# Value pages issued from GpSimd's queue, and value products spread over half projection tiles

## The chip, the cores and the metric

One Trainium2 chip, one core of it. The metric is the time of one execution on the device, in microseconds (us); lower is better. Engines are named as in the profile: PE (TensorE), DVE (VectorE), ACT (ScalarE), POOL (GpSimd), SP (SyncE, which here only issues DMAs).

## What is computed

One inference step of a hybrid decoder layer: 1024 prompt tokens, and 8 sample rows of one token, each of which has 4096 past tokens in a paged cache (32 pages of 128 tokens). The part that the change touches is this, cut from the reference:

```python
z = rmsnorm(x) @ w_in                      # one combined projection, split into heads
# group A, prompt: causal differential attention, 8 heads
s1 = einsum('bqhd,bshd->bhqs', q1, k1) * scale; s2 = einsum(... q2, k2) * scale
out = einsum('bhqs,bshd->bqhd', softmax(s1) - lam * softmax(s2), v)
# group A, sample: the same over 32 gathered pages of cache_diff_k and cache_diff_v per row
# group B: an indexer (4 heads of 64) scores all tokens, top 256 are kept, attention over those
rel = relu(einsum('bqhd,bsd->bqhs', qi, ki)); score = einsum('bqhs,bqh->bqs', rel, wi)
_, idx = lax.top_k(score, 256)
```

After it come group B's attention, the output projection and the gates. Everything is float32.

## The kernel before

The program is a chain of stages with a barrier between them. The change lies in the second one, which takes from about 262 to 1909 us of the profile. It runs in nine **slots**, s = 0 to 8. Slot s projects head s of group A for the prompt (slot 8: group B's keys and values), and does three other things beside that projection: the prompt attention of head s-1, the score products of sample row s with its 32 key pages and its indexer keys, and the value products of sample row s-1 with its 32 value pages.

A slot is cut into eight **tiles** t = 0 to 7 of 128 prompt tokens. In tile t PE does `scores` (L1277) of the attention, then the projections of two blocks, each in two halves (`half`, L1244, eight k-steps, 16 matmul records), then `output` (L1297), with `probabilities` (L1288, transposes) and `values` (L1316, the products with one value page) between them. Where the value products stand is set by the table `VALUES`. Names used below for the places in a tile: **a** is behind the first half of the first block, **b** behind its second half, **c** behind the first half of the second block, **d** at the tile's end behind `output`. Before, a row of the table gives the products at b, at c and at d.

Value pages sit in a ring of three buffers (`ring_v`), key pages in a ring of four (`ring_k`). A value page v waits on `v_used[v % 3]`, which PE raises behind the products of page v-3. A key page p waits on `k_used[p % 4]`, which DVE raises behind the reduction of page p-4. SP issues both, in one program order: behind key page i+4 comes value page i+3, then the next pair, with the weights of the next slot and the stores between them. So when SP stands at a value page whose buffer PE still holds, the key pages behind it wait too.

On DVE, `page(s, p)` multiplies key page p with the query (L958; for 12 of 32 pages POOL does it, L794) and then reduces page p-1 (L962) and the index product of page p-1 (L965). How many pages a tile does is in `PAGES`: in slots 1 to 7 tiles 1 to 7 do 5, 5, 6, 4, 4, 5 and 3 pages. The first page of a tile stands between `maxima` (L1078, of the scores) and `combine` (L1087 to L1090, which needs the exponentials from ACT); the others behind `combine` and, in tiles 1 to 4, behind `update`, five short steps of a bisection for group B's threshold.

On POOL, product u of the indexer keys (L800) waits on `q_free[u % 2]`, which DVE raises behind the reduction of product u-2:

```python
if 16 * s + u // 2:
    pool.wait_ge(q_free[u % 2], 16 * s + u // 2)
pool.tensor_tensor(kprod[:, u % 2, :, :], kib[:, j % 2, :, :], ...).then_inc(q_rdy[u % 2], 1)
```

The bisection takes 31 rounds; a round is one `counts` on ACT (L858, six passes) and one `update` on DVE. `ROUNDS_IN` spreads them over the slots. After the last, DVE does `settle` and one `select` for each tile from 2 to 7. `turned` (L840) on ACT copies the transposed queries and keys of the next slot out of PSUM; the next slot's `scores` wait for it.

## Time and profile before

| | us |
|---|---|
| median of 3 runs | 3952.08 (3949.98 to 3962.9) |
| the profiled execution, its own time | 3954.57 |
| its span, first to last instruction | 3952.8 |
| slots 1 to 7 of the stage, 432.3 to 1736.5 | 1304.2 |
| slot 8, 1736.5 to 1898.1 | 161.6 |

The profiled execution stands 2.5 us above the median, within the spread of the runs. A timeline row gives the start, the length, the engine, the line, the output and inputs, the count, and in brackets how long the engine had been idle and what ended that. A row of windows gives the stretch, its length, the busy time of PE, PE's weight loads, DVE, ACT and POOL, each with its count of instructions, the granted TensorE clock as a share of full speed, the share of DMA time in use, and GB/s.

### The profile page before, as it was taken

The numbers are of one execution on the slowest core, as the hardware profiler recorded it, in microseconds if no ns is written. First come the engines' busy times: TensorE is split into PE (matmuls) and PEld (weight loads), VectorE is DVE, ScalarE is ACT, GpSimd is POOL, SyncE is SP. The second block draws the span as 40 slices with busy tenths as digits, with TensorE's granted clock in tenths as the row PEclk, the third lists the DMA queues.
The fourth block names the chain that finished last, engine by engine and source line by source line (L and its number), as shares of the span: only waits on it lengthen the run. The fifth ranks groups of instructions, "written<-read, shape, count | busy, mean of one in ns | idle before, by whom it ended". The sixth has DMA issues, their size and how long they took to land. (4 is left out here: it accounts for less than half of the span.)

```text
span 3952.8 us, 46957 instructions
## 1 busy us (share of the span) xinstructions
PE 3453.9 (87%) x16995; PEld 2339.6 (59%) x17025; DVE 1497.0 (38%) x2771; ACT 820.3 (21%) x1798; POOL 514.0 (13%) x480
## 2 busy tenths in 40 slices
PE   4969789898988888889358699999979999899999
PEld 3757567676766666667223677777744444444443
DVE  2028666666666676654555111111110002311111
ACT  4011424141423333221000122222220001110000
POOL 0004333333333232310000200000000000000000
PEclk9989899998999999999669699999989999999999
DMA  9864676666666766754100211111041101310110
GB/s 341 253 192 145 189 259 195 226 213 223 222 224 217 226 224 200 242 163 135 53 0 9 77 27 28 27 28 27 10 156 43 43 22 53 113 59 32 59 59 22
DMA packets 344067, 497.51 MB, mean 126 GB/s; under 512 B 58913, under 2 KB 244538, under 8 KB 342674
## 3 DMA queue, kind: packets, MB, share of 16 engines
q1 hardware_dynamic: 338384, 481.67, 38.3%
q10 hardware_dynamic: 3922, 8.65, 0.6%
q0 software_dynamic: 1536, 4.20, 0.4%
q8 instruction: 141, 2.31, 0.2%
q14 instruction: 84, 0.69, 0.1%
HBM read 466.55 MB, written 27.90 MB: 125 GB/s over the span
## 5 line engine op out<-in xcount | busy, mean ns | idle before, releaser
L1244 PE MATMUL Z<-W,hT 128*128 128x256 f32 x4608 | 1063.8, 389 | 37.7 <-ACT qk L829 24.1
L1244 PEld LDWEIGHTS Z<-W,hT 128*128 128x128 f32 x4608 | 887.7, 196 | 165.3 <-ACT qk L829 26.5
L2138 PE MATMUL S<-W,hT 128*128 128x512 f32 x1408 | 646.1, 597 | 8.1 <-DMA hT<-oT_d 8.1
L2138 PEld LDWEIGHTS S<-W,hT 128*128 128x128 f32 x1408 | 264.9, 191 | 356.0 <-issue 346.9
L800 POOL TENSOR_TENSOR kprod<-kib,qib 128x256 f32<-128x256 f32 x256 | 231.5, 908 | 696.8 <-DVE srel L965 554.2
L962 DVE TENSOR_REDUCE sc<-big 128x16 f32<-128x1024 f32 x256 | 309.7, 1210 | 0.5 <-DVE isc L999 0.3
L2138 PE MATMUL Z<-W,hT 128*128 128x512 f32 x640 | 303.6, 592 | 0.0
L794 POOL TENSOR_TENSOR big<-big,qb 128x1024 f32<-128x1024 f32 x96 | 231.9, 2416 | 274.6 <-DMA big<-in_cache_diff_k_dram 274.6
L1316 PE MATMUL DB<-big,ex 128*4 128x256 f32 (+1 forms) x2112 | 150.7, 397 | 109.1 <-DMA big<-in_cache_diff_v_dram 108.9
L958 DVE TENSOR_TENSOR big<-big,qb 128x1024 f32<-128x1024 f32 x160 | 197.6, 1235 | 126.4 <-DMA big<-in_cache_diff_k_dram 123.5
L2138 PEld LDWEIGHTS Z<-W,hT 128*128 128x128 f32 x640 | 121.5, 190 | 153.0 <-issue 152.6
L1799 PE MATMUL Z<-W,hT 128*128 128x256 f32 x896 | 209.9, 395 | 0.0
L1799 PE MATMUL DB<-W,hT 128*128 128x256 f32 x896 | 198.8, 380 | 0.0
L1799 PEld LDWEIGHTS Z<-W,hT 128*128 128x128 f32 x896 | 176.5, 200 | 25.3
L1799 PEld LDWEIGHTS DB<-W,hT 128*128 128x128 f32 x896 | 168.1, 190 | 21.7
L1078 DVE TENSOR_REDUCE small<-S 128x1 f32<-128x256 f32 (+7 forms) x128 | 90.9, 752 | 224.7 <-PE S L1280 224.7
L858 ACT ACTIVATE vg<-isc,small 128x384 bf16<-128x384 f32 (+1 forms) x186 | 163.9, 881 | 22.5 <-DVE small L1008 14.9
L1969 DVE SCALAR_TENSOR_TENSOR vg<-Z,small,vg 128x128 f32<-128x128 f32 x64 | 22.4, 351 | 359.2 <-PE Z L1851 359.0
L872 ACT ACTIVATE e<-S,small 128x256 f32<-128x256 f32 (+7 forms) x128 | 93.6, 736 | 277.0 <-issue 275.3
L1316 PEld LDWEIGHTS DB<-big,ex 128*4 128x4 f32 (+1 forms) x2112 | 40.1, 85 | 176.9 <-DMA big<-in_cache_diff_v_dram 132.7
L1277 PE MATMUL S<-qkT 64*128 64x128 f32 (+3 forms) x576 | 107.0, 508 | 25.6 <-ACT qkT L840 23.3
L1277 PEld LDWEIGHTS S<-qkT 64*128 64x128 f32 x576 | 61.6, 237 | 89.5 <-issue 83.3
(539 smaller groups left out, 3305.5 us busy)
## 6 DMA issues: line engine op xcount, KB each, us to landing
big<-in_cache_diff_k_dram SPq DMA_DIRECT2D x256, 512.0 KB, 5.5
big<-in_cache_diff_v_dram SPq DMA_DIRECT2D x256, 512.0 KB, 5.0
W<-in_w_in_dram SPq DMA_DIRECT2D x27, 2048.0 KB, 10.0
W<-in_w_in_dram SPq DMA_DIRECT2D x52, 1024.0 KB, 7.3
W<-in_w_ple_gate_dram SPq DMA_DIRECT2D x16, 1024.0 KB, 5.1
W<-in_w_out_dram SPq DMA_DIRECT2D x12, 1024.0 KB, 5.1
kib<-in_cache_idx_k_dram SPq DMA_DIRECT2D x256, 32.0 KB, 2.3
hT<-oT_d SPq DMA_DIRECT2D x3, 2048.0 KB, 21.5
```

Of the source, the lines that this page charges most:

```text
L794: pool.tensor_tensor(ring_k[u % 4], ring_k[u % 4], qb[:, :], ALU.mult).then_inc(k_mul[u % 4], 1)
L800: pool.tensor_tensor(kprod[:, u % 2, :, :], kib[:, j % 2, :, :], spread(qib[:, h, :], 1, 4), ALU.mult).then_inc(q_rdy[u % 2], 1)
L858: act.activation(junkb(s, r)[:, 0:w], score(t), ACT.Sign, scale=-1.0, bias=thrf[:, t:t + 1], accum_out=ssum[:, t:t + 1]).then_inc(a_cnt, 1)
L872: act.activation(e12[:, j, 0:n], S[j][:, 0:n], ACT.Exp, scale=SC_A, bias=nmx[:, t, j:j + 1], accum_out=rsum[:, t, j:j + 1]).then_inc(s_fre ...
L958: dve.tensor_tensor(ring_k[p % 4], ring_k[p % 4], qb[:, :], ALU.mult).then_inc(k_mul[p % 4], 1)
L962: dve.tensor_reduce(sc[:, u, :], ring_k[u % 4].rearrange("p (g d) -> p g d", d=64), AX.X, ALU.add).then_inc(k_used[u % 4], 1)
L1078: last = dve.tensor_reduce(mx[:, t, j:j + 1], S[j][:, 0:n], AX.X, ALU.max)
L1244: mm = pe.matmul(Z[b][:, 0:CW], hT[:, k, t * P:(t + 1) * P], W[:, w, k, :], start=(k == 0), stop=(k == KT - 1))
L1277: pe.matmul(S[j][:, lo:hi], qkT[64 * j:64 * j + 64, 0, t * P:n], qkT[64 * j:64 * j + 64, 1, lo:hi], start=True, stop=(hi < n))
L1316: mm = pe.matmul(DB[32 * g:32 * g + 4, 0:256], ex[0:r, v, 4 * g:4 * g + 4], ring_v[v % 3][0:r, 256 * g:256 * g + 256], start=(v == 0), sto ...
L1799: mm = pe.matmul(PB[t % 2][:, 0:CW], hT[:, k, t * P:(t + 1) * P], W[:, u, k, :], start=(k == 0), stop=(k == KT - 1))
L2138: mm = pe.matmul(b, hT[:, k, t * P:(t + 1) * P], Wr[:, k, :], start=(k == 0), stop=(k == KT - 1))
```

## The change

It has five parts. (1) `VALUES` now has four places for each tile, a to d: two value products in tile 1 and five (1, 1, 1, 2) in each of tiles 2 to 7; before they stood in groups of two to four. (2) All value pages are issued from POOL's queue. In slots 1 to 7 the first three of a row stand at the slot's start; a later page v is issued ahead of the first index product u for which a planned time of page v-3 (`value_done`) is under the planned time of product u (`key_done`) less 0.8 of a tile. In slot 8 they are issued as buffers come free. (3) SP keeps the key pages, the index pages, the weights and the stores; the weights of the next slot and the key store stand at planned times. (4) Slot 0 does no bisection round where it did two, slot 8 does three where it did one; `settle` moves from tile 1 to tile 3 and `select(t)` to two tiles later, the last three all in tile 7. (5) `turned(0)` stands ahead of ACT's last copy of slot 0, and the semaphore of the value stores is split.

```diff
-        VALUES = ((0, 0, 0), (0, 0, 4), (2, 0, 3), (2, 0, 3), (0, 2, 3), (0, 2, 3), (0, 2, 3), (0, 2, 1))
-        ROUNDS_IN = (2,) + (4,) * (HA - 1) + (1,)
+        VALUES = ((0, 0, 0, 0), (0, 0, 0, 2)) + ((1, 1, 1, 2),) * 6
+        key_done = lambda s: [t + (0.35 if n == 0 else 0.5 + 0.5 * n / PAGES[s][t]) for t in range(NT) for n in range(PAGES[s][t])]
+        value_done = [t + 0.25 * (q + 1) for t in range(NT) for q in range(4) for n in range(VALUES[t][q])]
+        def transfers(s):
+            keys = [(u, 0, p + 4) for p, u in enumerate(key_done(s)) if p + 4 < NPG] if s < HA else []
+            return sorted(keys)
+        ROUNDS_IN = (0,) + (4,) * (HA - 1) + (3,)
...
             def _(sp):
...
-                    if s:
-                        for v in range(3):
-                            value_page(s - 1, v)
                     weights(s, 1)
...
-                    for i in range(NPG):
-                        if s < HA:
-                            if i % 4 == 0 and i + 4 < NPG:
-                                index_pages(s, i // 4 + 1)
-                            if i + 4 < NPG:
-                                key_page(s, i + 4)
-                        if s and i + 3 <= NPG:
-                            value_page(s - 1, i + 3)
-                        if i == 18 and s + 1 < SLOTS:
-                            weights(s + 1, 0)
-                        if i == 25:
-                            store_keys(s)
+                    due = [(4.1, lambda: weights(s + 1, 0))] if s + 1 < SLOTS else []
+                    due.append((5.6, lambda: store_keys(s)))
+                    for u, kind, n in transfers(s):
+                        while due and due[0][0] < u:
+                            due.pop(0)[1]()
+                        if kind == 0:
+                            if n % 4 == 0:
+                                index_pages(s, n // 4)
+                            key_page(s, n)
...
             def _(pool):
...
+                def value_page(b, v):
+                    n = 11 * b + v // 3
+                    if n:
+                        pool.wait_ge(v_used[v % 3], n)
+                    if v < NPG:
+                        page = pool.value_load(ptab[0:1, b * NPG + v:b * NPG + v + 1], min_val=0, max_val=POOL - 1)
+                        pool.dma_start(ring_v[v % 3], cv[ds(page, 1), :, :].rearrange("o p d -> (o p) d")).then_inc(v_rdy[v % 3], 16)
...
+                for s in range(SLOTS):
+                    if s:
+                        for v in range(3):
+                            value_page(s - 1, v)
+                    if s == HA:
+                        for v in range(3, NPG + 1):
+                            value_page(s - 1, v)
+                        break
                     pool.wait_ge(c_in, 32 * s + 32)
+                    issued = 3
                     for u in range(NPG):
+                        while s and issued <= NPG and value_done[issued - 3] < key_done(s)[u] - 0.8:
+                            value_page(s - 1, issued)
+                            issued += 1
...
                 for c in range(2 * NT):
+                    if c == 2 * NT - 1:
+                        turned(0)
                     take(0, c)
...
                         if s == HA:
-                            if t == 1:
+                            if t == 3:
                                 settle()
-                            if t >= 2:
-                                select(t)
+                            if t >= 4:
+                                select(t - 2)
                             if t == NT - 1:
+                                select(NT - 2)
+                                select(NT - 1)
                                 dve.nop().then_inc(d_sel, 1)
```

POOL, slot 2, from the slot's start. Here L800 before and L817 now are the index products, L794 and L811 the key page multiplications; L788 and L789 are a value page: the load of its page number, then its DMA. Before:

```order
L800 TENSOR_TENSOR kprod<-kib,qib 128x256 x2
L794 TENSOR_TENSOR big<-big,qb 128x1024
L800 TENSOR_TENSOR kprod<-kib,qib 128x256 x3
L794 TENSOR_TENSOR big<-big,qb 128x1024
L800 TENSOR_TENSOR kprod<-kib,qib 128x256 x2
L794 TENSOR_TENSOR big<-big,qb 128x1024
L800 TENSOR_TENSOR kprod<-kib,qib 128x256 x3
```

The same place now, behind the three pages of the slot's start:

```order
L817 TENSOR_TENSOR kprod<-kib,qib 128x256 x2
L811 TENSOR_TENSOR big<-big,qb 128x1024
L817 TENSOR_TENSOR kprod<-kib,qib 128x256 x3
L811 TENSOR_TENSOR big<-big,qb 128x1024
L817 TENSOR_TENSOR kprod<-kib,qib 128x256 x2
L811 TENSOR_TENSOR big<-big,qb 128x1024
L817 TENSOR_TENSOR kprod<-kib,qib 128x256 x2
L788 TENSOR_LOAD ptab
L788 ISA x2
L789 ISA
L789 DMA big<-in_cache_diff_v_dram 128x1024
```

Nine products, 0 to 8, stand ahead of the issue of value page 3. By the same rule pages 8, 13, 18, 23 and 28 stand behind products 13, 18, 22, 27 and 30.

PE, slot 1, tile 3 (L1277 and L1296 are scores, L1244 and L1263 projection halves, L1288 and L1307 transposes of the probabilities, L1297 and L1316 now the output, L1316 before and L1335 now the value products, four matmuls for each page). Before:

```order
L1277 MATMUL S<-qkT 128x384 x2
L1277 MATMUL S<-qkT 128x128 x2
L1280 MATMUL S<-causal,identb 128x128 x2
L1244 MATMUL Z<-W,hT 128x256 x16
L1316 MATMUL DB<-big,ex 4x256 x8
L1288 MATMUL TB<-ident,e 128x128 x4
L1244 MATMUL Z<-W,hT 128x256 x16
L1297 MATMUL Z<-vg,pT 128x128 x4
L1316 MATMUL DB<-big,ex 4x256 x12
```

Now:

```order
L1299 MATMUL S<-causal,identb 128x128 x2
L1263 MATMUL Z<-W,hT 128x256 x8
L1335 MATMUL DB<-big,ex 4x256 x4
L1263 MATMUL Z<-W,hT 128x256 x8
L1335 MATMUL DB<-big,ex 4x256 x4
L1307 MATMUL TB<-ident,e 128x128 x4
L1263 MATMUL Z<-W,hT 128x256 x8
L1335 MATMUL DB<-big,ex 4x256 x4
L1263 MATMUL Z<-W,hT 128x256 x8
L1316 MATMUL Z<-vg,pT 128x128 x4
L1335 MATMUL DB<-big,ex 4x256 x8
```

The five pages of tile 3 stood in two groups, two at b and three at d; now one each stands at a, b and c, and two at d. In tile 2 the page at b is page 3, in tile 3 page 8, and so on up to page 28 in tile 7.

## Rows read from the trace of the kernel before

**Rows 1.** Busy time, clock, DMA in windows: slot 1, slot 2, slot 8.
```profile
432.30:611.60 179.30, 162.50 (x999) 126.21 (x999) 115.20 (x177) 58.12 (x131) 56.61 (x51) 0.94 0.70 223
611.60:798.60 187.00, 167.82 (x1011) 130.87 (x1011) 119.30 (x186) 59.59 (x134) 59.97 (x51) 0.92 0.69 220
1736.50:1898.10 161.60, 157.21 (x1011) 125.38 (x1011) 85.81 (x160) 42.54 (x99) 0.00 (x0) 0.99 0.40 130
```

**Rows 2.** Waits, 448 to 1900 us: engine, line, releaser; total us, times, longest.
```profile
DVE big L958 <- DMA big<-in_cache_diff_k_dram: 119.8, 35, 6.5
...
PE DB L1316 <- DMA big<-in_cache_diff_v_dram: 108.9, 41, 5.7
```

**Rows 3.** Timeline of slot 2, PE, tiles 1 to 3 (start us, length us).
```profile
648.34 1.04 PE L1316 MATMUL DB<-big,ex 128*4 128x256 f32 x8 [3.57 <-DMA big<-in_cache_diff_v_dram]
...
649.31 1.65 PE L1277 MATMUL S<-qkT 64*128 64x256 f32 x8
...
651.08 8.82 PE L1244 MATMUL Z<-W,hT 128*128 128x256 f32 x32
...
661.20 3.62 PE L1244 MATMUL Z<-W,hT 128*128 128x256 f32 x16
...
676.56 9.75 PE L1244 MATMUL Z<-W,hT 128*128 128x256 f32 x32 [4.05 <-ACT qk L829]
```

**Rows 4.** Timeline of slot 2, DVE and POOL, tiles 2 and 3.
```profile
660.30 0.41 DVE L965 TENSOR_REDUCE srel<-kprod 128x4 f32<-128x256 f32 x1
...
660.95 1.48 POOL L800 TENSOR_TENSOR kprod<-kib,qib 128x256 f32<-128x256 f32 x1 [0.24 <-DVE srel L965]
...
685.44 0.41 DVE L965 TENSOR_REDUCE srel<-kprod 128x4 f32<-128x256 f32 x1
...
688.56 1.42 POOL L800 TENSOR_TENSOR kprod<-kib,qib 128x256 f32<-128x256 f32 x2
```

**Rows 5.** Windows over four tiles (3 to 6) of slot 2 and of slot 8.
```profile
671.15:773.94 102.79, 87.53 (x536) 66.76 (x532) 63.68 (x92) 26.82 (x64) 35.45 (x27) 0.90 0.73 234
1794.68:1875.43 80.75, 79.91 (x535) 62.72 (x531) 40.88 (x64) 15.50 (x39) 0.00 (x0) 1.00 0.43 143
```

**Rows 6.** The page's groups of key page and index product instructions.
```profile
L800 POOL TENSOR_TENSOR kprod<-kib,qib 128x256 f32<-128x256 f32 x256 | 231.5, 908 | 696.8 <-DVE srel L965 554.2
...
L962 DVE TENSOR_REDUCE sc<-big 128x16 f32<-128x1024 f32 x256 | 309.7, 1210 | 0.5 <-DVE isc L999 0.3
...
L794 POOL TENSOR_TENSOR big<-big,qb 128x1024 f32<-128x1024 f32 x96 | 231.9, 2416 | 274.6 <-DMA big<-in_cache_diff_k_dram 274.6
...
L958 DVE TENSOR_TENSOR big<-big,qb 128x1024 f32<-128x1024 f32 x160 | 197.6, 1235 | 126.4 <-DMA big<-in_cache_diff_k_dram 123.5
```

**Rows 7.** The page's DMA issues: size, median us from issue to landing.
```profile
big<-in_cache_diff_v_dram SPq DMA_DIRECT2D x256, 512.0 KB, 5.0
...
W<-in_w_in_dram SPq DMA_DIRECT2D x52, 1024.0 KB, 7.3
...
qib<-zs_d SPq DMA_DIRECT2D x8, 128.0 KB, 2.6
...
W<-in_cache_dsa_k_dram,qkT POOLq DMA_INDIRECT x16, 2.9
```

**Rows 8.** Timeline from slot 0 to slot 1, DVE and PE.
```profile
422.97 0.41 DVE L965 TENSOR_REDUCE srel<-kprod 128x4 f32<-128x256 f32 x1
...
432.34 0.80 PE L1277 MATMUL S<-qkT 64*128 64x128 f32 x4 [23.30 <-ACT qkT L840]
...
441.61 0.27 PE L1350 MATMUL DB<-ident,small 128*16 128x128 f32 x1
```

**Rows 9.** Timeline at the end of slot 8: DVE.
```profile
1884.33 0.75 DVE L1064 TENSOR_SCALAR big<-isc,small 128x1024 f32<-128x1024 f32 x1
...
1892.25 0.69 DVE L1071 TENSOR_SCALAR isc<-qb 128x1024 bf16<-128x1024 f32 x1
...
1897.08 0.35 DVE L1098 SCALAR_TENSOR_TENSOR vg<-Z,small,vg 128x128 f32<-128x128 f32 x1 [4.14 <-PE Z L1297]
```

More of the change, by code:

```diff
@@ L760, in _ @@
                         sp.dma_start(sc[0:1, NPG, :], snew_a_d[s:s + 1, :]).then_inc(row_in, 16)
[L761 to L772 removed]
+                    due = [(4.1, lambda: weights(s + 1, 0))] if s + 1 < SLOTS else []
[7 more added lines that the diff above has]
+                            key_page(s, n)
+                    for _, late in due:
+                        late()
                 store_values(SLOTS - 1)
                 sp.wait_ge(st_k, 16 * SLOTS)
[L775 removed]
+                sp.wait_ge(st_v, 16 * HA)
+                sp.wait_ge(st_sv, 16 * HKV)
             @block.gpsimd
@@ L786, in _ @@
                 link = Chain(pool, g_ch)
-                for s in range(HA):
+                def value_page(b, v):
[5 more added lines that the diff above has]
+                        pool.dma_start(ring_v[v % 3], cv[ds(page, 1), :, :].rearrange("o p d -> (o p) d")).then_inc(v_rdy[v % 3], 16)
+                    else:
+                        pool.dma_start(ring_v[v % 3][0:1, :], zs_d[b:b + 1, VA:VA + 1024]).then_inc(v_rdy[v % 3], 16)
+                for s in range(SLOTS):
[6 more added lines that the diff above has]
+                        break
                     pool.wait_ge(c_in, 32 * s + 32)
+                    issued = 3
                     for u in range(NPG):
+                        while s and issued <= NPG and value_done[issued - 3] < key_done(s)[u] - 0.8:
+                            value_page(s - 1, issued)
+                            issued += 1
                         if u in POOL_PAGES:
@@ L803, in _ @@
                             pool.nop().then_inc(i_used[j % 2], 1)
+                    for v in range(issued, NPG + 1 if s else 0):
+                        value_page(s - 1, v)
                     for b in range(2):
@@ L909, in _ @@
                         relu(*PAIRS[c])
-                    if c >= 2 * NT - ROUNDS_IN[0]:
-                        counts(0, c - 2 * NT + ROUNDS_IN[0])
-                turned(0)
                 for s in range(1, SLOTS):
@@ L1176, in _ @@
                             rotate(0)
-                for r in range(ROUNDS_IN[0]):
-                    update(r)
                 for s in range(1, SLOTS):
@@ L1321, in values, with some @@
                         pe.nop().then_inc(db_full, 1)
+                def some(s, v, n):
+                    for q in range(n):
+                        values(s, v + q)
+                    return v + n
                 def columns(s):
@@ L1344, in _ @@
                             columns(s - 1)
+                        v = some(s, v, VALUES[t][0])
                         half(s, 2 * t, 1)
@@ L1350, in _ @@
                             pe.transpose(DB[0:16, 256:384], m16, ident[:, :]).then_inc(db_full, 1)
-                        for n in range(pre):
-                            values(s, v + n)
-                        v += pre
+                        v = some(s, v, VALUES[t][1])
                         if t < 4:
@@ L1369, in _ @@
                             probabilities(s, t, 0)
-                            for n in range(mid):
-                                values(s, v + n)
-                            v += mid
+                        v = some(s, v, VALUES[t][2])
+                        if t >= 4:
                             probabilities(s, t, 1)
@@ L1379, in _ @@
                         output(s, t)
-                        for n in range(post):
-                            values(s, v + n)
-                        v += post
+                        v = some(s, v, VALUES[t][3])
                     values(s, NPG)
```

17 lines of the change are left out of this document (4 added, 13 removed).

## The prediction

> **What bounds the kernel now.** I read the stage in windows of slots first [rows 1]. PE is busy for 168 of 187 us in slot 2 and for 157 of 162 in slot 8. Slot 8 does nearly the same work on PE, but has no key pages and no index products. So slots 1 to 7, 1304 us in all by the table, lose time that is not PE's work. The four tiles 3 to 6 show it closer [rows 5]: 102.8 us in slot 2 at a granted clock of 0.90, 80.8 us in slot 8 at 1.00. The waits say what is late [rows 2]: PE waited 108.9 us for value pages and DVE 119.8 us for key pages. One engine issues both in one order, and a value page whose buffer is still in use holds the keys behind it.
>
> In the timeline of slot 2 [rows 3], tile 1 ends with four value products over three buffers, and the fourth page comes 3.6 us late. The 32 projection records behind that wait took 8.8 us where 16 take 3.6 at full clock, so the wait cost a further 1.6 us in slow clock. The 4.1 us wait for ACT in tile 3 is followed by 9.8 us for 32 records, 2.5 us slow. I take 2 us of slow clock behind each wait.
>
> **What POOL's order does.** This is the part on which my forecast rests. A value page now stands behind an index product in POOL's program. Product u can't start before DVE has reduced product u-2. DVE does that at a fixed place in its tile, behind the maxima of the tile's scores and, from the second page on, behind the exponentials and `combine`. By the order, page 3, which PE wants at b of tile 2, stands behind product 8, so behind the reduction of page 6, the second one behind `combine` in tile 2. The trace has both [rows 3, 4]: tile 2 starts at 649.3, the reduction of page 6 ends at 660.7, product 8 ends at 662.4, so 13.1 us into the tile. PE wants the page after scores (1.8 us), two halves (7.2) and the product at a (0.5): 9.5 us. The page isn't even issued then. Its buffer was free at the tile's start.
>
> In tile 3, page 8 stands behind product 13. The reduction of page 11 that frees product 13 ends at 685.9, 14.7 us into the tile that started at 671.15 [rows 4, 5]; product 13, behind POOL's own multiplication of page 13, ended at about 18 [rows 4]. With key pages on time that multiplication (2.4 us [rows 6]) starts at about 13 and I get 16.2.
>
> The same happens in tiles 4 to 7. I worked the time from tile start to the end of the product that stands ahead of page 13, 18, 23 and 28, with key pages on time: scores and maxima (3.3 to 4.5 us, by the tile's width), the first page, which is a multiplication 1.2, a reduction 1.2 and an index reduction 0.4 [rows 4, 6], `combine` about 2, `update` 1 in tile 4, and then as many pages as the order puts ahead, and a product of 0.7 to 0.9. That gives 12.3, 11.1, 14.7 and 7.0. In tile 7 page 28 needs only the tile's first page, hence the short one.
>
> From product end to landing I take 6.2 us: page number and issue 0.5 (my estimate), landing 5.0 [rows 7], 0.3 for POOL's way (128 KB took 2.9 us from POOL, 2.6 from SP [rows 7]), and 0.4 because two pages are issued together. A plain 512 KB issue from POOL is nowhere in this trace. Its bounds are 5.5, SP's landing and nothing for POOL, and 12, twice what I take.
>
> | tile | page | landing | wanted at, undisturbed | late |
> |---|---|---|---|---|
> | 2 | 3 | 19.3 | 9.5 | 9.8 |
> | 3 | 8 | 22.4 | 8.9 | 13.5 |
> | 4 | 13 | 18.5 | 9.2 | 9.3 |
> | 5 | 18 | 17.3 | 9.6 | 7.7 |
> | 6 | 23 | 20.9 | 9.6 | 11.3 |
> | 7 | 28 | 13.2 | 9.8 | 3.4 |
>
> Late in a slot: 55.0 us. In tile 3 the ACT wait and its slow clock lie inside the 13.5. The other pages come in time: the second of a pair lands 1.5 us behind the first and PE wants it 4.5 us later, and the two at d have over 10 us. Behind b a tile has some 11 us of work left, in which DVE ends its pages, so the next tile starts with the key ring full, and lateness neither adds up nor melts away. It comes once for each tile.
>
> **The sum.** An undisturbed slot: slot 8's 161.6, less 3.6 + 1.6 for the wait in tile 1, which has two products now instead of four, is 156.4. Plus 55.0, plus six slow clocks of 2: 223.4. Seven slots make 1564. Slot 1 has less ACT delay in tile 3; I take off 3: 1561 against 1304, so +257.
>
> Slot 0 to 1 [rows 8]: PE idles 23.3 us, to 432.3, for ACT, which does two `counts` ahead of `turned(0)`. Both are gone. PE now starts slot 1 at about 409, but runs into DVE: the last page of slot 0 ends at 423.4, maxima, the key maximum and `combine` take until 427.5, and what stood at 441.6 can stand there. So -14, not -23. The key reductions are the cover that sets this.
>
> Slot 8: no products gate POOL there. The spread products save the 5 us of tile 1. Three rounds instead of one bring the ACT wait of tile 3 (4 + 2) into it. In tile 7 DVE now does three selects. The one of 1024 columns took 1884.3 to 1892.9, 8.6 us [rows 9]; those of 768 and 896, by their columns, some 6.5 and 7.5. They end 22.6 behind 1884.3, at 1907, where the last `natural` now starts at 1897.1: +10, and +1 for the last store behind `turned`. Slot 8 in all: -5 + 6 + 11 = +12. The smaller selects and `settle` in earlier tiles lie under the projection.
>
> The other edits I cost at nothing: the places of the weights and the key store on SP move by a page or two, with most of a slot before the weights are needed; the store's split semaphore waits for transfers of the slot before. If that cover were gone, it would be one 7.3 us weight load a slot [rows 7]. SP gives up 33 issues a slot and isn't waited for on them any more. POOL is busy for 60 of 187 us [rows 1] and has room for 33 issues, even at 3 us each.
>
> Sum: 3954.6 - 14 + 257 + 12 = 4209.6 for an execution like the profiled one. That one is 2.5 above the median, so 4207.
>
> **A rule against a row.** The landing of a 512 KB page is 5.0 us in the row [rows 7]. The Trainium skill, DMA: Bandwidth & Descriptors, section "Anatomy of one DMA", fits transfers from GpSimd with 2.0 us plus the bytes over 436 GB/s, by which a page lands in 3.2 us; an estimate by that fit takes 1.8 x 6 x 7 = 76 us off the sum. The row was taken under this kernel's traffic, so I stay with it.
>
> **The rivals.**
>
> *The waits go away* (faster). Value pages no longer hold key pages, the products are spread, and PE gets every page in time. For it: the 108.9 and 119.8 us of waits, and slot 8, which runs like that. A slot would take 156.4 + 6 for ACT = 162.4, seven of them 1137, less 3 in slot 1, so -170, and the time is 3952 - 14 - 170 + 12 = 3780. Against it: product 8 would have to be done by 3.3 us into tile 2 for page 3 to land by 9.5, and the trace has it at 13.1. It decides if DVE runs more than two pages ahead of where the trace has it, which its own program order forbids.
>
> *One late wait for another* (same). SP's issue time is saved, POOL's is paid, and the late pages cost what the old waits did. A slot now loses 187 - 162 = 25 us; mine loses 67 - 6 beyond 162. Each late page would have to land 6 us sooner than in my table. Time 3950. The Trainium skill, same page, section "Issuing engines are not separate DMA queues", says that spreading issues over engines saves only the issue time. Taken alone it gives this outcome; it doesn't weigh the program order, which the table is about.
>
> *POOL's issues are dear* (slower still). Where descriptors are made by POOL itself, a page may land 12 us behind the product, which adds 5.8 x 6 x 7 = 244: 4450. For it: the trace has no 512 KB issue from POOL, and one that takes POOL 3 us would delay the second page of each pair and the products behind it as well. Against it: 2.9 against 2.6 us for the same 128 KB [rows 7]. The Trainium skill, SBUF — State Buffer, section "SBUF: two separate sides", says that a transfer issued from GpSimd can't get its descriptors written while VectorE runs an operation in its two-port mode. No run here shows it.
>
> **How the numbers follow.** My forecast 0.84, dear issues 0.06, same 0.03, waits gone 0.07. Likeliest 4207. Its range: if pages land at 5.0 behind the product and the clock costs 1 us instead of 2, a slot is 13.2 us shorter, -92, and if tile 3 runs some 3 us sooner, 4095. If the key pages stay as late as they are in slot 2, the products of tiles 3 to 7 end 18 us later in a slot, +126: 4333. So 4095 to 4335, which leaves out the other cases and hardly more. A measurement of this kernel can tell 0.3% from no change. Faster 0.07, same 0.03, slower 0.90.
>
> **What would show it.** PE's wait for value pages at b of tiles 2 to 7, 8 to 13 us each in tiles 2 to 6, some 350 us in total where it was 109; each released by a page that POOL issued right behind an index product, with its buffer long free. DVE's wait for key pages mostly gone. Slots of about 223 us, slot 8 near 163 plus the selects. PE's wait before slot 1 no longer for ACT. Pages from POOL landing in 5 to 6 us. Wrong if product 8 ends within 5 us of tile 2's start, or if a page from POOL lands in 3 us, or if the key pages are still late.

## The result, and the profile after

The changed kernel takes 4262.72 us (median of 4 runs, 4259.55 to 4265.34), against 3951.67 us for the kernel before (4 runs): a ratio of 1.078, 95% interval 1.0759 to 1.0802. It is slower by 311 us. The forecast was 4207, range 4095 to 4335.

Windows of the changed kernel: slot 1, slot 2, slot 8, tiles 3 to 6 of slot 2, and slots 2 to 7 together; they answer to [rows 1, 5].

```profile
409.06:650.60 241.54, 172.28 (x1000) 129.84 (x1000) 131.40 (x191) 58.47 (x132) 86.22 (x97) 0.84 0.57 183
650.60:881.83 231.23, 173.00 (x1011) 131.05 (x1012) 120.31 (x186) 59.58 (x134) 77.87 (x84) 0.87 0.56 178
2029.99:2205.36 175.37, 161.00 (x1011) 124.02 (x1011) 87.90 (x171) 52.16 (x119) 17.95 (x33) 0.96 0.38 117
718.16:855.50 137.34, 92.97 (x534) 68.18 (x530) 64.66 (x92) 27.12 (x66) 44.71 (x46) 0.83 0.54 176
650.60:2029.99 1379.39, 1035.51 (x6067) 784.50 (x6067) 721.47 (x1116) 357.47 (x804) 465.19 (x504) 0.87 0.56 179
```

A slot of 2 to 7 takes 1379.39 / 6 = 229.9 us where it took 187.5. PE's own work is the same in count; DMA moves less each us (178 against 220 GB/s). Everything waits more. For what, the waits of the changed kernel from 420 to 2230 us say (total us, times, longest), beside [rows 2]:

```profile
POOL kprod L817 <- DVE srel L984: 619.4, 118, 11.5
...
PE DB L1335 <- DMA big<-in_cache_diff_v_dram: 369.3, 42, 16.6
...
PE Z L1263 <- ACT qk L848: 31.6, 7, 4.5
...
DVE big L977 <- DMA big<-in_cache_diff_k_dram: 1.8, 4, 1.0
```

DVE's wait for key pages is gone, 119.8 to 1.8 us. PE's wait for value pages more than tripled, and its count of 42 is six in each of seven slots. PE's timeline shows which six; here the two of tiles 2 and 3 of slot 2, which start at 683.23 and 718.16, and the one of tile 6, which starts at 815.32:

```profile
683.23 0.92 PE L1296 MATMUL S<-qkT 64*128 64x256 f32 x8
...
704.07 1.03 PE L1335 MATMUL DB<-big,ex 128*4 128x256 f32 x8 [11.99 <-DMA big<-in_cache_diff_v_dram]
...
705.73 5.79 PE L1263 MATMUL Z<-W,hT 128*128 128x256 f32 x16
...
724.06 5.25 PE L1263 MATMUL Z<-W,hT 128*128 128x256 f32 x16 [4.54 <-ACT qk L848]
...
740.44 1.04 PE L1335 MATMUL DB<-big,ex 128*4 128x256 f32 x8 [6.94 <-DMA big<-in_cache_diff_v_dram]
...
841.06 1.03 PE L1335 MATMUL DB<-big,ex 128*4 128x256 f32 x8 [16.04 <-DMA big<-in_cache_diff_v_dram]
```

Each stands at b of its tile. POOL, in the same stretch:

```profile
696.52 1.57 POOL L817 TENSOR_TENSOR kprod<-kib,qib 128x256 f32<-128x256 f32 x1 [0.79 <-DVE srel L984]
698.04 0.58 POOL L789 DMA_DIRECT2D big<-in_cache_diff_v_dram  x1
```

Page 3 is issued at 698.04, 14.8 us into tile 2, straight behind the index product that waited for DVE's reduction, and PE uses it 6.0 us later. Page 0, which holds the same buffer, is used up at the end of tile 1, before 683.23. So for 14.8 us the page waited for nothing but the instructions ahead of it in POOL's program.

### The profile page after: what moved, and what is told of

Its sections match the earlier page's. It is cut to its first block and busy times, and to the rows that moved or that the text cites. A ratio compares the mean times of both kernels' runs of the same rounds, so it can differ in the third digit from the quotient of the medians.

```text
span 4262.6 us, 47002 instructions
## 1 busy us (share of the span) xinstructions
PE 3508.1 (82%) x17025; PEld 2349.2 (55%) x17025; DVE 1502.4 (35%) x2771; ACT 819.7 (19%) x1798; POOL 660.7 (16%) x744
## 5 line engine op out<-in xcount | busy, mean ns | idle before, releaser
L1263 PE MATMUL Z<-W,hT 128*128 128x256 f32 x4608 | 1132.9, 403 | 45.0 <-ACT qk L848 31.6
L1263 PEld LDWEIGHTS Z<-W,hT 128*128 128x128 f32 x4608 | 912.0, 203 | 231.7 <-issue 55.1
L1335 PE MATMUL DB<-big,ex 128*4 128x256 f32 (+1 forms) x2112 | 166.2, 410 | 369.3 <-DMA big<-in_cache_diff_v_dram 369.3
L817 POOL TENSOR_TENSOR kprod<-kib,qib 128x256 f32<-128x256 f32 x256 | 237.0, 927 | 768.2 <-DVE srel L984 691.8
L1335 PEld LDWEIGHTS DB<-big,ex 128*4 128x4 f32 (+1 forms) x2112 | 34.9, 84 | 436.0 <-DMA big<-in_cache_diff_v_dram 386.1
L1117 DVE SCALAR_TENSOR_TENSOR vg<-Z,small,vg 128x128 f32<-128x128 f32 x64 | 22.4, 351 | 637.7 <-PE Z L1316 637.3
L811 POOL TENSOR_TENSOR big<-big,qb 128x1024 f32<-128x1024 f32 x96 | 227.3, 2367 | 13.6 <-DMA big<-in_cache_diff_k_dram 13.0
L789 POOL DMA_DIRECT2D big<-in_cache_diff_v_dram x256 | 143.2, 559 | 508.0 <-issue 399.0
L977 DVE TENSOR_TENSOR big<-big,qb 128x1024 f32<-128x1024 f32 x160 | 212.5, 1328 | 6.7 <-DMA big<-in_cache_diff_k_dram 4.1
L1819 PE MATMUL Z<-W,hT 128*128 128x256 f32 x896 | 210.0, 395 | 0.0
L2158 PEld LDWEIGHTS Z<-W,hT 128*128 128x128 f32 x640 | 122.1, 191 | 154.1 <-issue 153.6
L1819 PEld LDWEIGHTS Z<-W,hT 128*128 128x128 f32 x896 | 176.5, 200 | 25.2
L901 ACT ACTIVATE pT<-TB 128x512 f32<-128x512 f32 (+2 forms) x96 | 47.0, 489 | 597.7 <-PE TB L1307 597.7
L1989 DVE SCALAR_TENSOR_TENSOR vg<-Z,small,vg 128x128 f32<-128x128 f32 x64 | 22.4, 351 | 359.4 <-PE Z L1871 359.2
```

The lines of the kernel that those rows point to most:

```text
L789: pool.dma_start(ring_v[v % 3], cv[ds(page, 1), :, :].rearrange("o p d -> (o p) d")).then_inc(v_rdy[v % 3], 16)
L811: pool.tensor_tensor(ring_k[u % 4], ring_k[u % 4], qb[:, :], ALU.mult).then_inc(k_mul[u % 4], 1)
L977: dve.tensor_tensor(ring_k[p % 4], ring_k[p % 4], qb[:, :], ALU.mult).then_inc(k_mul[p % 4], 1)
L1263: mm = pe.matmul(Z[b][:, 0:CW], hT[:, k, t * P:(t + 1) * P], W[:, w, k, :], start=(k == 0), stop=(k == KT - 1))
L1335: mm = pe.matmul(DB[32 * g:32 * g + 4, 0:256], ex[0:r, v, 4 * g:4 * g + 4], ring_v[v % 3][0:r, 256 * g:256 * g + 256], start=(v == 0), sto ...
L1819: mm = pe.matmul(PB[t % 2][:, 0:CW], hT[:, k, t * P:(t + 1) * P], W[:, u, k, :], start=(k == 0), stop=(k == KT - 1))
```

## The experiments

Each kernel was timed in three rounds beside the kernel before, whose medians were 3954 to 3956 us; ratios are to those. They stand in the order in which they are best read.

**1. The lead shortened (e1_lag03).** In the changed kernel, value pages stand 0.3 of a tile, not 0.8, ahead of the product by which POOL's order counts them due:

```diff
-                        while s and issued <= NPG and value_done[issued - 3] < key_done(s)[u] - 0.8:
+                        while s and issued <= NPG and value_done[issued - 3] < key_done(s)[u] - 0.3:
```

> The changed kernel with the planned lead of 0.8 of a tile set to 0.3, so value pages stand some three to four index products earlier in POOL's order. Theory (the program order on POOL holds the page back until DVE's second page of the tile): the 369 us of PE waits for value pages go to under 40, slots 1 to 7 take about 165 us instead of 230, time about 3808 us. Rival (a page issued from POOL is dear in itself, by descriptor making or by stalling POOL's products): the waits stay with PE or move to DVE for index products, time above 4100 us.

Measured: 3864.46 us, ratio 0.9767 (0.9746 to 0.9788). One number in POOL's order takes 398 us off, though not all that I expected: the time is 56 us above my 3808, and PE's wait is 52 us where I had under 40. PE's waits, and POOL's for the buffers that PE holds, from 420 to 2230 us:

```profile
POOL big L789 <- PE DB L1335: 158.9, 29, 30.6
...
PE DB L1335 <- DMA big<-in_cache_diff_v_dram: 51.8, 20, 4.9
```

The issues are the same in number, engine and size; only their place differs. The theory of the place holds. That value issues from POOL would be the loss in themselves doesn't.

**2. Products spread, SP's issues left alone (e2_spread_sp).** The kernel before with the new `VALUES`, nothing else:

```diff
-        VALUES = ((0, 0, 0), (0, 0, 4), (2, 0, 3), ...)
+        VALUES = ((0, 0, 0, 0), (0, 0, 0, 2)) + ((1, 1, 1, 2),) * 6
```

> The kernel before with only the value products spread to places a, b, c and d; SP issues all pages in the old order. Theory (spreading is harmless and even good, the loss is in where POOL issues): PE's 109 us of waits for value pages shrink to under 60, DVE still waits over 80 us for key pages that stand behind value pages, time 3880 us, between 3830 and 3940. Rival (spreading the products costs in itself, by more switches on PE): 3955 us or more.

Measured: 3876.26 us, ratio 0.98 (0.9781 to 0.9818). The waits of this kernel from 420 to 2230 us:

```profile
DVE big L958 <- DMA big<-in_cache_diff_k_dram: 248.4, 84, 6.9
...
PE DB L1316 <- DMA big<-in_cache_diff_v_dram: 15.8, 11, 2.0
```

Spreading alone takes PE's wait from 108.9 to 15.8 us and gains 79 us, as expected. DVE waits longer for keys than before (248.4 against 119.8), and the time falls all the same: it was PE's wait that was paid.

**3. The rounds and selects alone (e3_rounds_only).** The kernel before with `ROUNDS_IN`, `settle`, `select` and `turned(0)` as in the change:

```diff
-        ROUNDS_IN = (2,) + (4,) * (HA - 1) + (1,)
+        ROUNDS_IN = (0,) + (4,) * (HA - 1) + (3,)
```

> The kernel before with only the bisection rounds moved from slot 0 to slot 8, settle and the selects later, and the copy of the turned queries ahead of ACT's last copy of slot 0. Theory (my terms: -14 before slot 1, +6 for ACT in slot 8, +11 for the three selects at the end): 3955 us, within 6 us of the kernel before. Rival (the bigger part of the 1.2% that the result lies over my figure is here): 3985 us or more.

Measured: 3965.55 us (9 runs), ratio 1.0029 (1.0019 to 1.0039), 9.7 us above the kernel before beside it (3955.86). The profiled execution is the fastest of the nine; its span is 3958.2 us, 5.4 above the span before. Slot 1 starts at 410.26 instead of 432.34, and slot 8, with its three rounds and its late selects, takes 180.7 us (1718.93 to 1899.6) instead of 161.6, so the two ends of the stage nearly cancel, and some 10 us are left on the wrong side. I had expected to be within 6 us, so this lies a little outside, and far below the rival's 3985.

**4. Only the b pages moved (e4_b_pages).** As experiment 1, but the short lead only for pages 3, 8, 13, 18, 23 and 28:

```diff
-                        while s and issued <= NPG and value_done[issued - 3] < key_done(s)[u] - 0.8:
+                        while s and issued <= NPG and value_done[issued - 3] < key_done(s)[u] - (0.3 if issued % 5 == 3 else 0.8):
```

> The changed kernel with the lead of 0.3 only for the six pages of a slot that PE wants at b (3, 8, 13, 18, 23, 28); the others keep 0.8. Theory: the wait moves from b to c, since the next page now stands alone behind the same product, and is shorter by the half and the issue between them, some 5.5 us for each page: PE's waits about 160 us, time about 4055 us. Rival (the wait comes from the landing of pages from POOL in general): the waits stay near 370 us and the time within 1% of 4263.

Measured: 4114.37 us, ratio 1.0413 (1.0386 to 1.044). PE waits 225.6 us, 68 times. The wait moved one product on: page 4, wanted at c and still behind its old index product, is now late by 7.8 us on average in tile 2, page 24 by 10.9 in tile 6. The pages at b were the first late ones, not the only ones. I had expected 4055 and 160 us of waits: one page late in each tile, by 5.5 us less than before. In tiles 2 and 6 that is near (11.9 less 5.5 is 6.4, measured 7.8; 15.9 less 5.5 is 10.4, measured 10.9). But of the 225.6 us 192 are at c, and 33 us, in 33 shorter waits, are at d, where I had none.

**5. Selects back into earlier tiles (e5_selects).** As experiment 1, and slot 8 does `select` as the tiles allow:

```diff
-                            if t >= 4:
-                                select(t - 2)
-                            if t == NT - 1:
-                                select(NT - 2)
-                                select(NT - 1)
+                            for q in {4: (2, 3), 5: (4, 5), 6: (6,), 7: (7,)}.get(t, ()):
+                                select(q)
```

> The run with the lead of 0.3, and the selects of slot 8 in tiles 4 (2 and 3), 5 (4 and 5), 6 (6) and 7 (7) instead of three in tile 7. Theory (the three selects in tile 7 set the stage's end, 13 to 16 us late): 3864 less 14, so 3850 us, with the last natural of slot 8 starting about 22 us behind the tile's start. Rival (the end is set by something else, the stores): 3862 us or more.

Measured: 3846.85 us, ratio 0.9727 (0.971 to 0.9745), 17.6 us under experiment 1. Of the 15.3 us between the two spans (3861.5 and 3846.2), 2.5 lie in the slots before, 8.9 in slot 8 (174.0 against 165.2, its start to its last `natural`), and the rest behind it: this prices the three selects in the last tile.

**6. Lead 0.1 (e6_lag01).** As experiment 5 with 0.1 in place of 0.3.

> As the run before it, with the lead at 0.1, so that pages 6, 12 and 26, which were still late at 0.3, stand one to three products earlier. Theory: PE's waits for value pages fall from 52 us to about 25 us and the time to about 3830 us. Rival (POOL now stands at pages whose buffer is in use and DVE runs out of index products): DVE's waits for POOL grow and the time is 3850 us or more.

Measured: 3820.85 us, ratio 0.9665 (0.9648 to 0.9683). PE's wait for value pages is 9.3 us. The largest row that is left in the stage is ACT's copy in tile 3, 31.6 us, 7 times, as in the changed kernel.

**7. All pages from SP at the planned times (e7_sp_planned).** As experiment 5, but with value pages sorted into SP's one order beside the key pages:

```diff
-            return sorted(keys)
+            values = [(u + 0.02, 1, v + 3) for v, u in enumerate(value_done) if v + 3 <= NPG] if s else []
+            return sorted(keys + values)
```

> As the run with the selects spread, but SP issues the value pages too, each at the planned time at which its buffer comes free, sorted in with the key pages; POOL issues none. Theory (what counts is the place in program order, not which engine issues): about 3855 us, within 1% of the run with POOL at a lead of 0.3. Rival (POOL's queue is what gains, SP blocks keys behind values however they are sorted): 3885 us or more.

Measured: 4000.14 us, ratio 1.0125 (1.0106 to 1.0143). My expectation of 3855 fell, and the time lies in the rival's range, by which SP holds keys behind values however they are sorted. Experiment 8 tells the two apart. PE waits for value pages (124.5 us), and SP's queue, from 420 to 1990 us, shows why it might:

```profile
SPq L703 <- PE DB L1326: 274.8, 75, 21.7
SPq L694 <- DVE sc L974: 244.9, 64, 11.8
```

L694 is a key page's wait for DVE's reduction (L974). `page(p)` on DVE reduces page p-1, so a key buffer comes free one page later than this plan has it. SP stands there, and the value pages behind it wait as well.

**8. The explanation tested (e9_sp_keys_late).** Experiment 7 with each key page planned at the step that really frees its buffer:

```diff
-            keys = [(u, 0, p + 4) for p, u in enumerate(key_done(s)) if p + 4 < NPG] if s < HA else []
+            done = key_done(s) + [NT] if s < HA else []
+            keys = [(done[p + 1], 0, p + 4) for p in range(NPG - 4)] if s < HA else []
```

> e7 with one change: a key page's planned time is that of the step in which its buffer is really released (the reduction of page p is made in the step of page p+1, so one page later than e7 planned). Theory (in e7's one queue the value pages stood behind key pages that were put one step too early, and waited there for DVE's reduction): PE's wait for value pages falls from 124 us to under 40 us, and the time from 4000 to about 3870 us. Rival (the queue's plan is not the point: SP's issues themselves, or DMA traffic, make e7 slow): within 20 us of e7, 3980 to 4020. Second rival (the lateness moves over to the keys: DVE waits more than it did): between, about 3930.

Measured: 3841.91 us, ratio 0.9711 (0.9695 to 0.9727), 158 us less for one place in an order. SP's row for the same wait, and PE's:

```profile
SPq L695 <- DVE sc L975: 86.2, 44, 3.6
...
PE DB L1327 <- DMA big<-in_cache_diff_v_dram: 30.1, 18, 6.0
```

DVE's wait for key pages rose from 55.1 to 134.1 us, as the second rival had it, but the time is far from that rival's 3930. This stands within 5 us of experiment 5, which has the same work and issues the value pages from POOL. So it matters little here which engine issues, and much in which order.

**9. Old groups, issued from POOL (e8_groups_pool).** Experiment 5 with the value products in groups as before:

```diff
-        VALUES = ((0, 0, 0, 0), (0, 0, 0, 2)) + ((1, 1, 1, 2),) * 6
+        VALUES = ((0, 0, 0, 0), (0, 0, 0, 4), (0, 2, 0, 3), (0, 2, 0, 3), (0, 0, 2, 3), (0, 0, 2, 3), (0, 0, 2, 3), (0, 0, 2, 1))
```

> As the run with the selects spread, but with the value products in their old groups (4, then 2 and 3 in a tile), issued from POOL at a lead of 0.3. Theory (spreading gives each page at least half a tile between buffer free and use, groups do not): PE's waits for value pages near the 109 us of before or above, DVE's waits for key pages near zero, time about 3900 us. Rival (spreading is worth nothing once POOL issues): 3850 us.

Measured: 4041.64 us, ratio 1.0226 (1.0204 to 1.0247), worse than the 3900 that I expected. PE waits 211.8 us, 80 times, longest 9.1. My reading, which no run tests, is that with groups over three buffers a page is wanted soon after its buffer comes free, twice in a tile, and that each such place meets an index product in POOL's order. With this lead, moving the issues to POOL without spreading loses; spreading alone gains (experiment 2).

**10. Twice as many issues (e10_halves).** Experiment 6 with each value page as two DMAs of 64 rows:

```diff
-                        pool.dma_start(ring_v[v % 3], ...).then_inc(v_rdy[v % 3], 16)
+                        for c in (0, 64):
+                            pool.dma_start(ring_v[v % 3][c:c + 64, :], ...).then_inc(v_rdy[v % 3], 16)
```

> e6 (3821 us) with each value page issued by POOL as two DMAs of 64 rows and 256 KB each, so 33 more issues a slot. It prices a plain issue on POOL's queue. Theory (an issue costs POOL about 0.6 us, POOL has the time, and a page lands at most 1 us later): 33 x 0.6 = 20 us more of POOL's time in each slot, of which a few us at most reach PE: 3820 to 3845. Rival (issues from POOL are dear, 3 us or more with the descriptors, so that my forecast's rival of dear issues would have been near): each of the 231 further issues delays what stands behind it, above 3950.

Measured: 3917.31 us, ratio 0.99 (0.9883 to 0.9917), 96 us above experiment 6 and between my two expectations. An issue costs POOL little: the 256 further ones keep it 135 us (0.53 each), spread over the stage. Most of the 96 us shows elsewhere. Windows over slots 2 to 7 and the page's landing times, first experiment 6:

```profile
580.87:1596.28 1015.41, 970.62 (x6067) 746.80 (x6067) 784.43 (x1116) 357.78 (x804) 451.78 (x504) 0.98 0.76 243
...
big<-in_cache_diff_k_dram SPq DMA_DIRECT2D x256, 512.0 KB, 4.9
big<-in_cache_diff_v_dram POOLq DMA_DIRECT2D x256, 512.0 KB, 5.2
```

then this one:

```profile
602.88:1689.69 1086.81, 988.35 (x6066) 754.01 (x6067) 782.85 (x1116) 358.33 (x804) 542.54 (x702) 0.96 0.92 228
...
L790 POOL DMA_DIRECT2D big<-in_cache_diff_v_dram x512 | 270.5, 528 | 461.4 <-issue 451.6
...
big<-in_cache_diff_k_dram SPq DMA_DIRECT2D x256, 512.0 KB, 7.2
big<-in_cache_diff_v_dram POOLq DMA_DIRECT2D x512, 256.0 KB, 6.7
```

The DMA share goes from 0.76 to 0.92 while fewer GB/s are moved, and the key pages, which the edit leaves alone, land in 7.2 us instead of 4.9. DVE's wait for them rises from 30.5 to 142.5 us. Half a page takes longer to land than a whole one did, 1.5 us longer in the median where I had allowed 1. PE feels it in two rows: 41.1 us for value pages instead of 9.3, and this one, which in experiment 6 is 3.5 us:

```profile
PE TB L1307 <- DVE e L1111: 47.8, 11, 7.7
```

That is PE waiting for `combine`, which in DVE's order stands behind the first page of its tile.

**11. ACT's six passes split (e11_split_counts).** Experiment 6, and of the third round's six passes three stay in tile 2 and three go behind tile 3's exponentials:

```diff
                         exps(s, t)
+                        if t == 3:
+                            counts(s, 2, 5)
...
-                            counts(s, t)
+                            counts(s, t, 2, 5 if t == 2 else NT)
```

> e6 with the third round's six passes on ACT split: three in tile 2 as before, three in tile 3 behind the exponentials. In e6 PE waits 4.5 us in tile 3 of each slot for ACT's copy behind those passes, 31.6 us in all, and this is the largest wait of PE left in the stage. Theory (that wait is on the path): 3.3 us of passes no longer stand ahead of the copy, so 3 to 4.5 us a slot less over 8 slots: 3790 to 3798. Rival (the passes now delay the copy of the second block, and the wait only moves): 3815 to 3825.

Measured: 3794.94 us, ratio 0.9596 (0.9578 to 0.9613). The wait of 31.6 us shrinks to 7.1, and the time falls by 26: it was on the path.

**12. Earlier still (e12_early).** Experiment 11 with `+ 0.1` in place of `- 0.1`.

> e11 (3795 us) with the lead turned round, from 0.1 of a tile to minus 0.1: value pages stand still earlier in POOL's order, some ahead of the planned time at which PE frees their buffer. Theory (a page in POOL's order has two ways to be wrong; now POOL stands at it and the index products behind wait, which DVE and then the key pages feel): PE's wait for value pages falls below the 19 us of e11, POOL's wait for PE's buffers rises above its 153 us, DVE starts to wait for index products, and the time rises, to 3800 to 3850. Rival (earlier is always better until DVE waits, and DVE has slack): 3780 to 3795. Above 3950 would say that a page too early costs as much as a page too late.

Measured: 3790.46 us (3784.98 to 3798.97), ratio 0.9589 (0.9569 to 0.961). No different from experiment 11 (3791.54 to 3802.23), so the rival was right: this order, 0.2 of a tile earlier, costs nothing measurable. PE waits for no value page at all in slots 2 to 7. Instead DVE waits 90.2 us for POOL's multiplications, and the time doesn't show it. One sign that I had named went the other way: POOL's wait for the buffers that PE holds fell, from 152.9 to 73.2 us, where I had it rise. I don't know why.

## Why the forecast was right, and where its sizes were off

**The place in POOL's order** was the step the forecast rested on, and it is shown: by the 42 waits, by their release, and by experiments 1 and 6, which change nothing but the place (6 beside 5). The late pages by tile, as forecast, and as PE's timeline has them on average in slots 2 to 7:

| tile, page | product end, forecast / measured (us into tile) | product end to use, measured (forecast 6.2) | late, forecast | PE's wait, measured |
|---|---|---|---|---|
| 2, page 3 | 13.1 / 14.8 | 5.9 | 9.8 | 11.9 |
| 3, page 8 | 16.2 / 17.8 | 4.8 | 13.5 with ACT's wait | 6.5 + 4.5 for ACT |
| 4, page 13 | 12.3 / 14.1 | 5.1 | 9.3 | 9.9 |
| 5, page 18 | 11.1 / 11.4 | 4.0 | 7.7 | 5.9 |
| 6, page 23 | 14.7 / 16.7 | 8.9 | 11.3 | 15.9 |
| 7, page 28 | 7.0 / 7.0 | 4.4 | 3.4 | 1.5 |
| sum | | | 55.0 | 56.1 |

The sum is right to 1.1 us, and that is in part luck: two errors cancel. The products end up to 2 us later than I had them, and in every tile but the sixth the page is used sooner behind its product than the 6.2 us that I took. Page 23 in tile 6 is the one that I undersized most, by 4.6 us: 2.0 at the product's end and 2.7 behind it. (In tile 3 the two columns don't hold quite the same: my 13.5 has the slow clock behind ACT's wait in it, the 6.5 + 4.5 has not.)

The late products have a collision in them that I didn't price. Here it is in tile 2 of slot 2, then the same step of `update` in tile 3 without it, then `combine` in tiles 4 and 6:

```profile
689.44 2.35 POOL L811 TENSOR_TENSOR big<-big,qb 128x1024 f32<-128x1024 f32 x1 [0.94 <-DMA big<-in_cache_diff_k_dram]
689.48 2.33 DVE L1047 TENSOR_TENSOR small<-small 128x8 int32<-128x8 int32 x1
...
727.46 0.17 DVE L1047 TENSOR_TENSOR small<-small 128x8 int32<-128x8 int32 x1
...
759.56 2.34 POOL L811 TENSOR_TENSOR big<-big,qb 128x1024 f32<-128x1024 f32 x1
759.65 2.94 DVE L1109 SCALAR_TENSOR_TENSOR e<-e,small 128x640 f32<-128x640 f32 x1
...
822.96 2.34 POOL L811 TENSOR_TENSOR big<-big,qb 128x1024 f32<-128x1024 f32 x1
823.05 3.21 DVE L1109 SCALAR_TENSOR_TENSOR e<-e,small 128x896 f32<-128x896 f32 x1
...
833.32 0.57 POOL L789 DMA_DIRECT2D big<-in_cache_diff_v_dram  x1 [1.30 <-issue]
```

A step on 128x8 elements that starts 0.04 us behind a multiplication on POOL took 2.33 us instead of 0.17, and ends with the multiplication. `combine` on 640 columns took 2.94 us where it took 0.89 in the kernel before, and on 896 it took 3.21 and ends at 826.26, 1.0 us behind the end of POOL's multiplication (825.30): as if it had waited for the whole of it. The same instruction on 1024 columns took 1.28 us at 2179.66 in slot 8, where POOL has nothing to multiply. So tiles 2, 4 and 6 lose about 2 us each, and these 2 us go straight into the reduction, the product and the page. In tile 3 it is POOL's product 13 that takes 1.76 us, beside a multiplication on DVE, where 0.74 is usual:

```profile
734.71 1.21 DVE L977 TENSOR_TENSOR big<-big,qb 128x1024 f32<-128x1024 f32 x1
734.74 1.76 POOL L817 TENSOR_TENSOR kprod<-kib,qib 128x256 f32<-128x256 f32 x1
```

The kernel before had the collision of tile 6 already, and not that of tile 4:

```profile
1645.19 0.89 DVE L1090 SCALAR_TENSOR_TENSOR e<-e,small 128x640 f32<-128x640 f32 x1
...
1694.55 3.20 DVE L1090 SCALAR_TENSOR_TENSOR e<-e,small 128x896 f32<-128x896 f32 x1
```

The Trainium skill, SBUF — State Buffer, section "SBUF: two separate sides", says that an operation of VectorE with two inputs in SBUF and one of GpSimd take turns at a shared port, each for its whole instruction; by that rule, the trace agrees.

**From product to landing** I took 6.2 us. 0.9 of it (0.5 for page number and issue, 0.4 for two pages together) came from no row, and the 0.3 for POOL's way compared a gather from POOL with a plain load from SP. The issue is cheap, as I took it, but has two parts. The page's group and landing of the changed kernel:

```profile
L789 POOL DMA_DIRECT2D big<-in_cache_diff_v_dram x256 | 143.2, 559 | 508.0 <-issue 399.0
...
big<-in_cache_diff_k_dram SPq DMA_DIRECT2D x256, 512.0 KB, 4.7
big<-in_cache_diff_v_dram POOLq DMA_DIRECT2D x256, 512.0 KB, 5.4
```

0.56 us for the issue, and where issues stand together some 0.55 idle before the next, in which the order has the load of the page number. The landing of 5.4 is 5.0 plus 0.4; I had 5.0 and 0.3. Beside the key pages of the same trace, it is 0.7 more. The median hides a spread: behind its issue page 18 is used after 4.0 us, page 23 after 7.6. Page 23 is issued 1.3 us behind its product where the others need 0 to 0.4, and from 812 to 860 us, where SP issues four key pages at the same time, all pages land late, the key pages after 7.6 us and the value pages so:

```profile
big<-in_cache_diff_v_dram POOLq DMA_DIRECT2D x5, 512.0 KB, 7.7
```

The rows settle the question of rule against row: the fit in the Trainium skill, DMA: Bandwidth & Descriptors, section "Anatomy of one DMA", gives 3.2 us for this transfer, and no kernel here had a median under 5.2 from POOL. The row decides.

**The sum of slots 1 to 7** was +257 and came out at +307.6, measured from tile 1 of slot 1 to slot 8 (1286.9 to 1594.5). This is the term that was mis-sized, and it is the undisturbed slot that was wrong, not the waits and not the clock. Windows of experiment 12, in which PE waits for no value page: slots 2 to 7, and slot 8.

```profile
583.81:1573.74 989.93, 962.44 (x6066) 738.55 (x6067) 733.86 (x1116) 358.00 (x804) 452.44 (x500) 0.99 0.77 249
1573.74:1734.70 160.96, 159.01 (x1011) 122.59 (x1011) 87.68 (x170) 54.36 (x123) 18.78 (x37) 1.00 0.44 136
```

In slots 2 to 7 PE is busy 160.4 us a slot here, at a clock of 0.99, and 172.6 in the changed kernel, at 0.87, with the same matmuls. The 12.2 us between them are what the slow clock cost: 2.0 behind each of six waits, as I took it. From the changed kernel's 229.9, less 12.2 and less the 56.1 of waits, 161.6 is left for the undisturbed slot, where I had 156.4. So +5.2 on the base, +1.1 on the waits, +0.2 on the clock: 6.5 a slot, 39 in six.

I had built 156.4 from slot 8 of the kernel before. Key pages are not what it lacked: slot 8 of experiment 12 has none either, and takes 161.0 us, 4.6 over my base. What it has is the new order. PE is busy 159.0 us in it, where in the old slot 8 it was busy 157.2, 1.6 of that being slow clock. The same matmuls stand in more pieces now, and pieces take longer, as these two rows show, of slot 8 before and of slot 8 in experiment 12:

```profile
1795.86 7.13 PE L1244 MATMUL Z<-W,hT 128*128 128x256 f32 x32
...
1628.70 3.72 PE L1263 MATMUL Z<-W,hT 128*128 128x256 f32 x16 [1.01 <-ACT qk L848]
```

Two pieces of 16 take 7.4 us, one of 32 takes 7.1. No run changes this alone, so that it makes up the larger part of the 5.2 is an estimate, from 159.0 against 155.6.

The other 12 of the missing 51 are in slot 1: 215.1 us from its tile 1 to slot 2, where I had 203.1 (220.4 for the slot, less the 17.3 that tile 0 took before). PE waits 60.1 us for value pages there, where I had 52.0, and 16.6 of it for page 3: product 8 ends 18.5 us into tile 2 instead of 14.8. Why it does in slot 1 is open. The clock of such a stretch is in the windows above: 0.83 in tiles 3 to 6, where PE idled a third of the time, 0.90 before.

**Slot 0 to 1** was -14. PE and DVE of the changed kernel:

```profile
423.32 1.04 DVE L1156 TENSOR_REDUCE small<-sc 128x16 f32<-128x528 f32 x1
...
424.41 0.38 PE L1375 MATMUL DB<-ident,small 128*16 128x128 f32 x1 [7.57 <-DVE small L1156]
```

As argued, PE now starts the slot at 409 and runs into DVE's key maximum (the row at 423.32). What stood at 441.6 [rows 8] stands at 424.4, and tile 1 of slot 1 starts at 435.5 instead of 449.6, so 14.1 sooner.

**Slot 8** was +12: it took 175.4 us by the window above against 161.6, +13.8, and 2.5 more pass until the stage ends, +16.3. Three selects stand behind each other in tile 7 (three of their first steps, then `natural`):

```profile
2180.87 0.61 DVE L1083 TENSOR_SCALAR big<-isc,small 128x768 f32<-128x768 f32 x1
...
2187.78 0.69 DVE L1083 TENSOR_SCALAR big<-isc,small 128x896 f32<-128x896 f32 x1
...
2195.57 0.75 DVE L1083 TENSOR_SCALAR big<-isc,small 128x1024 f32<-128x1024 f32 x1
...
2204.34 0.35 DVE L1117 SCALAR_TENSOR_TENSOR vg<-Z,small,vg 128x128 f32<-128x128 f32 x1 [0.16 <-DVE isc L1090]
```

6.9, 7.8 and 8.8 us, where I had 6.5, 7.5 and 8.6, and `natural` waits for the last of them. Experiment 5 takes this back.

-14.1 + 307.6 + 16.3 = 309.8, which is the difference of the two spans (4262.6 and 3952.8).

**The rivals.** "The waits go away" was the right picture of a kernel that is one number away, though not in its size: experiment 1 runs in 3864 where I gave it 3780. Experiment 12 runs in 3790, but with the edits of experiments 5 and 11 as well, which were worth 18 and 26 us, so that it comes near 3780 is luck. I wrote that it needs DVE more than two pages ahead. For the changed kernel that holds; what I didn't see is that a value page put further up in POOL's order does the same, with DVE where it is. "One late wait for another" fell with PE's wait for value pages, 369.3 us where it was 108.9. "Dear issues" fell with the landing of 5.4 us. That doubling the issues costs 96 us goes with slower landings for all pages, and not with a busier POOL.

**What stays open.** Why the old groups lose so much from POOL (experiment 9) was only argued. Why slot 1 is later than the others isn't known. Of the 4.6 us that PE still idles in each slot 2 to 7 of experiment 12, about half is the wait for `combine` on DVE (14.1 us in the six slots, 10 times), and most of the rest is for ACT; no run tests what they are worth.

## What to carry to other kernels

When a transfer is moved to another engine's queue, look for what stands ahead of it in that engine's program, follow that instruction's own wait to the engine that raises it, and put the time beside the one at which the data is wanted. A planned time that is off by one step of the other engine cost 158 us in SP's order, and a lead half a tile off cost 398 us in POOL's, so plan each transfer by the instruction that frees its buffer. And price an undisturbed stretch in the order that the new kernel will have: the same matmuls in the old order came out 5 us a slot too short.

## What the runs showed of the hardware

- Two transfers of 64 rows in place of one of 128 rows, the same bytes, took more of the DMA engines: POOL's queue had 15.4% of their time against 10.8%, and the transfers of SP's queue landed later (key pages 4.9 to 7.2 us, index pages 3.1 to 5.2).
- An operation on DVE that started up to 0.1 us behind a POOL multiplication of 2.3 us took about 2 us longer: `combine` 3.21 us on 896 columns and 2.94 on 640, against 1.28 on 1024 and 0.89 on 640 without one; a step on 128x8 elements 2.33 us against 0.17. In the other direction a product on POOL took 1.76 us against 0.74 when it started 0.03 us behind a multiplication on DVE.
- POOL's plain issue of 512 KB: 0.56 us, some 0.55 us idle before the next one, where the page number is loaded, and 5.2 to 5.8 us to landing in the medians of the eight kernels that issue whole pages from POOL, 0.3 to 1.0 us more than the key pages from SP in the same trace.
- Six waits of 1.5 to 16 us in a slot cost PE 12.2 us more in the same matmuls (172.6 us busy at a granted clock of 0.87, 160.4 at 0.99).
